# Delta-rule core: decode states by 32-wide TensorE tiles, and three inputs of an iteration made at the end of the one before

## What is computed

```
def step(s, xs):
    qk_i, qd_i, kd_i, u_i, w_i, gt_i = xs
    v_new = u_i - jnp.einsum('bhcd,bhde->bhce', w_i, s)
    o_i = jnp.einsum('bhcd,bhde->bhce', qd_i, s) + jnp.einsum('bhij,bhje->bhie', qk_i, v_new)
    s = s * gt_i[..., None, None] + jnp.einsum('bhcd,bhce->bhde', kd_i, v_new)
    return s, o_i
```

## Time and profile before

| | |
|---|---|
| median of 3 runs | 1932.04 us (1931.34 to 1932.73) |
| the profiled execution: its own time | 1922.21 us |
| its span | 1919.9 us |
| mean granted TensorE clock | 0.913 of 2.4 GHz |
| core stage, first L1028 to last L972 | 311.7 to about 841 us |

### The profile page before, as it was taken

One profiled execution on the slowest core, in us unless ns is written; L12 is line 12 of the kernel. 1 busy time (PEld: TensorE's weight loads), 2 busy tenths in 40 slices (PEclk: granted clock), 3 DMA queues, 4 the chain that ended last, 5 costly groups with the idle time before them and its releaser, 6 DMA issues. The chain is left out here.

```text
span 1919.9 us, 36793 instructions
## 1 busy us (share of the span) xinstructions
PE 1676.9 (87%) x13304; PEld 1389.8 (72%) x13304; DVE 922.1 (48%) x1578; ACT 769.4 (40%) x1572; POOL 210.9 (11%) x396
## 2 busy tenths in 40 slices
PE   4899849998998899979899999788777777899996
PEld 3899837654565566548799998787555556799996
DVE  2776275354434435435455552421556554556631
ACT  2676322334423433443255542331445442455621
POOL 0232000120210212010000000011111100000000
PEclk9899966999899999987999999895788986899998
DMA  7345230122212221242355666444434323355640
GB/s 178 108 135 161 77 102 28 50 69 83 79 37 82 79 61 56 67 115 69 107 139 146 161 164 146 121 139 138 159 104 157 125 94 88 88 153 143 179 121 27
DMA packets 283016, 208.09 MB, mean 108 GB/s; under 512 B 29087, under 2 KB 274751, under 8 KB 282448
## 3 DMA queue, kind: packets, MB, share of 16 engines
q1 hardware_dynamic: 273606, 174.22, 32.5%
q0 software_dynamic: 9248, 31.80, 5.2%
q10 hardware_dynamic: 42, 0.44, 0.1%
HBM read 183.57 MB, written 22.85 MB: 108 GB/s over the span
## 5 line engine op out<-in xcount | busy, mean ns | idle before, releaser
L509 PE MATMUL psum<-h_rounded,weights_low 128*128 128x320 f32 x1248 | 394.3, 316 | 30.0 <-DVE h_low_nsa L420 10.2
L509 PEld LDWEIGHTS psum<-h_rounded,weights_low 128*128 128x128 f32 x1248 | 236.4, 189 | 36.4 <-DVE h_low_nsa L420 10.7
L950 PE MATMUL psum<-sbuf_resident 128*128 128x504 f32 x512 | 254.6, 613 | 0.0
L511 PE MATMUL psum<-h_rounded,weights_high_wide 128*128 128x320 f32 x704 | 219.7, 312 | 0.0
L510 PE MATMUL psum<-h_low_ffn,weights_high_wide 128*128 128x320 f32 x704 | 218.4, 310 | 0.0
L511 PE MATMUL psum<-h_rounded,weights_high 128*128 128x320 f32 x544 | 167.8, 308 | 0.0
L584 DVE SCALAR_TENSOR_TENSOR sbuf_stages<-sbuf_stages,sbuf_resident 128x344 f32<-128x344 f32 (+1 forms) x184 | 105.6, 574 | 110.5 <-ACT sbuf_stages L566 106.6
L485 DVE TENSOR_TENSOR weights_low<-sbuf_resident,weights_high_wide 128x2048 fp32r<-128x2048 f32 (+1 forms) x60 | 149.6, 2499 | 14.5 <-ACT weights_high_wide L470 14.5
L983 ACT COPY sbuf_resident<-psum 64x256 f32<-64x256 f32 x256 | 93.8, 366 | 143.0 <-PE psum L943 140.4
L470 ACT CAST weights_high_wide<-sbuf_resident 128x2048 fp32r<-128x2048 f32 (+1 forms) x60 | 123.6, 2063 | 60.1 <-DMA sbuf_resident<-in_ffn_w_down_dram 60.1
L485 DVE TENSOR_TENSOR weights_low<-sbuf_resident,weights_high 128x2048 fp32r<-128x2048 f32 x46 | 105.1, 2291 | 82.3 <-ACT weights_high L470 82.3
(11 more groups left out here) (410 smaller groups left out, 3229.3 us busy)
## 6 DMA issues: line engine op xcount, KB each, us to landing
sbuf_resident<-in_ffn_w_up_dram SPq DMA_DIRECT2D x88, 512.0 KB, 4.9
sbuf_resident<-in_gdn_w_in_dram SPq DMA_DIRECT2D x48, 512.0 KB, 4.7
sbuf_resident<-in_ffn_w_down_dram SPq DMA_DIRECT2D x32, 704.0 KB, 6.2
sbuf_resident<-in_cache_nsa_kv_dram SPq DMA_DIRECT2D x256, 64.0 KB
sbuf_stages<-in_state_gdn_s_dram POOLq DMA_DIRECT2D x16, 512.0 KB, 5.3
out_gdn_s_sample_dram<-sbuf_stages SPq DMA_DIRECT2D x16, 512.0 KB, 3.5
sbuf_resident<-in_gdn_w_out_dram SPq DMA_DIRECT2D x16, 512.0 KB, 5.5
sbuf_stages<-in_cache_nsa_kv_dram POOLq DMA_DIRECT2D x64, 128.0 KB, 3.5
```

Of the source, the lines that this page charges most:

```text
L509: pe.matmul(out, w_lo, x_hi_tile, start=first, stop=False)
L511: return pe.matmul(out, w_hi, x_hi_tile, start=False, stop=last)
L950: last = pe.matmul(psum[:, H_BANK[t], 0:4 * NC2], w1[:, v, 8 * half + m, t * P:(t + 1) * P], blocks, start=(m == 0 and half == 0), stop=(m ...
```

## The change

Four edits, all in the core:

1. **Old states (L1104, now L1108).** Each 128x128 mask matmul becomes matmuls with 32 stationary columns: for each head, k or q (`x`) and sequences 0 to 3 or 4 to 7 (`e`) have their own quarter of 32 output partitions, and each quarter accumulates four sequences (`b`). 16 matmuls per head where there were 8. The masks shrink from 8 x 64 to 8 x 32 columns for each of k and q.
2. **New states (L1149, now L1154).** `spread` holds on its rows 0 to 31 sequences 0 to 3 and on rows 32 to 63 sequences 4 to 7, 512 columns in place of 1024; the two matmuls of a head use 32 rows each, rows 0 to 31 for one bank, rows 32 to 63 for the other.
3. **ACT copies k and q of iteration i+1 at the end of iteration i**, after the outputs and before the silu; the first pair before the loop. PE's first wait is for q instead of v1, and a wait for v is added before the transposes of v. POOL makes the masks first in its iteration, before the loads of states.
4. **DVE makes the two row products of iteration i+1 in iteration i**, when PE has done the outputs, before the additions of the new states; the first pair before the loop.

```diff
+    put("tok_four", t[:64, None] // TQ % 4 == b[None, :4])
+    put("spare", np.zeros((P, 1468)))
...
-            h["spread"] = space.take(NB, P, off=start)
+            h["spread"] = space.take(NB // 2, P, off=start)
...
-        kqmask = kmask_space.rearrange("p (b x c) -> p b x c", b=NB, x=2)
+        kqmask = kmask_space[:, 0:NB * 2 * 32].rearrange("p (e b x c) -> p e b x c", e=2, b=4, x=2)
...
-            dve=steps("core_dve", both(["row", "bts", "d", "cd", "at1"]) + ["atc", "ya", "yb", "x0"] + both(["at2"])
+            dve=steps("core_dve", both(["bts", "d", "cd", "at1"]) + ["atc", "ya", "yb", "x0"] + both(["at2"])
...
-                      + both(["rs", "vn0", "vns", "s1", "r1", "vn1", "s2"]) + both(["snew"]), lag=True),
-            act=steps("core_act", ["k", "q"] + both(["v"]) + ["ktok"] + both(["egc", "dec", "kdec", "r"]) + both(["qs"]) + both(["o"]), loop=True),
+                      + both(["rs", "vn0", "vns", "s1", "r1", "vn1", "s2", "row"]) + both(["snew"]), lag=True),
+            act=steps("core_act", both(["v"]) + ["ktok"] + both(["egc", "dec", "kdec", "r"]) + both(["qs"]) + both(["o"]) + ["k", "q"], lag=True),
             pool=steps("core_pool", ["kmask", "s0g0", "s0g1", "spread0", "spread1"], lag=True))
...
-            pe.wait_ge(act_steps.sem, act_steps.count("v1", i))
+            pe.wait_ge(act_steps.sem, act_steps.count("q", i - 1))
             pe.wait_ge(dve_steps.sem, dve_steps.count("qkd1", i - 1))
...
-            pe.wait_ge(dve_steps.sem, dve_steps.count("row1", i))
+            pe.wait_ge(dve_steps.sem, dve_steps.all_before(i))
...
+                pe.wait_ge(act_steps.sem, act_steps.count(f"v{h}", i))
                 pe.wait_ge(dve_steps.sem, dve_steps.count(f"p{LEVELS - 1}{h}", i))
...
-                for b in range(NB):
-                    last = pe.matmul(psum[:, B_BANK[h], 3 * P:4 * P], kqmask[:, b].rearrange("p x c -> p (x c)"), hd[h]["S0"][:, b, :],
-                                     start=(b == 0), stop=(b == NB - 1))
+                for b in range(4):
+                    for x in range(2):
+                        for e in range(2):
+                            last = pe.matmul(psum[64 * x + 32 * e:64 * x + 32 * e + 32, B_BANK[h], 3 * P:4 * P], kqmask[:, e, b, x, :],
+                                             hd[h]["S0"][:, 4 * e + b, :], start=(b == 0), stop=(b == 3))
...
                 for x, b in ((0, A_BANK[h]), (1, B_BANK[h])):
-                    last = pe.matmul(psum[:, b, :], d["kdec"][0:TS, 2, :],
-                                     d["spread"][0:TS, 4 * x:4 * x + 4, :].rearrange("p a b -> p (a b)"), start=True, stop=True)
+                    r = slice(32 * x, 32 * x + 32)
+                    last = pe.matmul(psum[:, b, :], d["kdec"][r, 2, :], d["spread"][r].rearrange("p a b -> p (a b)"), start=True, stop=True)
...
-            act.sem_inc(S5["act"].sem, 1)
+            act.sem_inc(S5["act"].sem, S5["act"].first - 2)
...
+            for x in ("k", "q"):
+                take(act, 0, x).then_inc(S5["act"].sem, 1)
...
+        def take(act, i, x):
+            if x == "k":
+                return act.copy(kS[:, 0:T], one(qkv[:, bass.ds(QKH + i, 1), :]))
+            return act.copy(qS, one(qkv[:, bass.ds(i, 1), :]))
+
         def act_core_pair(act, g, i, v):
             act_steps, dve_steps, pe_steps = S5["act"], S5["dve"], S5["pe"]
-
-            act.wait_ge(pe_steps.sem, pe_steps.count("o1", i - 1))
-            act.wait_ge(S5["pool"].sem, S5["pool"].count("kmask", i - 1))
-            act.copy(kS[:, 0:T], one(qkv[:, bass.ds(QKH + i, 1), :])).then_inc(act_steps.sem, act_steps.step("k"))
-            act.copy(qS, one(qkv[:, bass.ds(i, 1), :])).then_inc(act_steps.sem, act_steps.step("q"))
...
+            act.wait_ge(S5["pool"].sem, S5["pool"].count("kmask", i))
+            for x in ("k", "q"):
+                take(act, i + 1, x).then_inc(act_steps.sem, act_steps.step(x))
...
+        def rows_of(dve, i, h):
+            return dve.tensor_scalar(row_src[h], rows4[:, 0:2, :], ident[0:VH, bass.ds(2 * i + h, 1)], None, ALU.mult)
+
         def dve_core(dve):
             dve_steps, pe_steps, act_steps, pool_steps = S5["dve"], S5["pe"], S5["act"], S5["pool"]
-            dve.sem_inc(dve_steps.sem, dve_steps.first)
+            dve.sem_inc(dve_steps.sem, dve_steps.first - 4)
+            for h in range(2):
+                rows_of(dve, 0, h).then_inc(dve_steps.sem, 2)
...
-                for h in range(2):
-                    dve.wait_ge(pe_steps.sem, pe_steps.all_before(i))
-                    dve.tensor_scalar(row_src[h], rows4[:, 0:2, :], ident[0:VH, bass.ds(2 * i + h, 1)], None, ALU.mult).then_inc(dve_steps.sem, dve_steps.step(f"row{h}"))
...
+                    dve.wait_ge(pe_steps.sem, pe_steps.count(f"o{h}", i))
+                    rows_of(dve, i + 1, h).then_inc(dve_steps.sem, dve_steps.step(f"row{h}"))
...
+            pool.wait_ge(act_steps.sem, act_steps.count("q", i - 1))
+            for x, src in ((0, kS), (1, qS)):
+                four = const("col_seq").rearrange("p (b c) -> p b c", b=NB)[:, 0:4, 0:32]
+                last = pool.tensor_tensor(kqmask[:, :, :, x, :], four.unsqueeze(1).to_broadcast([P, 2, 4, 32]),
+                                          src[:, TP:T].rearrange("p (e c) -> p e c", e=2).unsqueeze(2).to_broadcast([P, 2, 4, 32]), ALU.mult)
+            last.then_inc(pool_steps.sem, pool_steps.step("kmask"))
             pool.wait_ge(state_out, STATES * i + 16)
             for h in range(2):
                 pool.dma_start(hd[h]["S0"], st[bass.ds(2 * i + h, 1)].rearrange("o k b v -> (o k) b v")).then_inc(state_in, 16)
-            pool.wait_ge(act_steps.sem, act_steps.count("q", i))
-            for x, src in ((0, kS), (1, qS)):
-                last = pool.tensor_tensor(kqmask[:, :, x, :], const("col_seq").rearrange("p (b c) -> p b c", b=NB),
-                                          src[:, TP:T].unsqueeze(1).to_broadcast([P, NB, TS]), ALU.mult)
-            last.then_inc(pool_steps.sem, pool_steps.step("kmask"))
...
-                pool.tensor_tensor(hd[h]["spread"][0:TS], hd[h]["vn"][0:TS, 2, :].unsqueeze(1).to_broadcast([TS, NB, P]),
-                                   const("tok_seq", TS).unsqueeze(2).to_broadcast([TS, NB, P]), ALU.mult).then_inc(pool_steps.sem, pool_steps.step(f"spread{h}"))
+                pool.tensor_tensor(hd[h]["spread"][0:TS], hd[h]["vn"][0:TS, 2, :].unsqueeze(1).to_broadcast([TS, 4, P]),
+                                   const("tok_four", TS).unsqueeze(2).to_broadcast([TS, 4, P]), ALU.mult).then_inc(pool_steps.sem, pool_steps.step(f"spread{h}"))
```

2 lines of the change are left out of this document (1 added, 1 removed).

## The result

The changed kernel takes 1867.32 us (median of 4 runs, 1863.5 to 1874.97) against 1931.69 us of the kernel before in the same comparison (four runs, 1919.97 to 1932.73). The ratio is 0.9685, with a 95% interval from 0.9637 to 0.9734: faster by 3.2%.

A forecast was written before the change was run, and what follows sets the result against it. PE was taken as the bound, idle only around iteration boundaries. Savings of 12.7, 14.2, 16.3, 3.8 and 3, less 0.3, make 49.7: 1922.2 becomes 1872.5, plus 9.8 gives 1882.3 us, range 1876 to 1896.

The forecast's parts named there:

- term 1: Old states (L1104): four column tiles at once, 1.98 us against 3.57 per iteration, 12.7 us saved; ends -2 to 14.
- term 2: New states (L1149): 32-row matmuls run in pairs, 1.77 us instead of 3.54 per iteration, 14.2 us saved; ends 0 to 14.2.
- term 3: Boundaries without a loop branch, into iterations 1, 3, 5, 7: no wait before the Gram products, 16.3 us saved.
- term 4: Boundaries with the loop branch, into iterations 2, 4, 6: the branch pause stays, 3.8 us saved.
- term 5: First small product to old states (L1054 to L1104): low-clock stretches and port stall mostly go, 3 us saved; ends 0 to 4.
- start and first iteration: Entry of the core stage: first start, like the last end, would move within 1 us.
- A: Old states: column tiles of full height run only two at once, saving about 0 instead of 12.7, total 1895 us; chance 0.09.
- D: Old and new states: small tiles don't overlap at all, old states 30.5 us longer, new states gain nothing, total 1940; chance 0.03.
- rival E: Odd boundaries: PE pauses for code there too, its program being longer, 3.3 us at each of four, total 1895; chance 0.04.
- rival B: Before the first small product (L1054): the ACT–DVE chain holds PE after all, 7.6 + 2.8 us less gain, total 1893; chance 0.14.
- rival C: After boundaries: two more stretches at 1.2 GHz and the last 3 us gain lost, total 1890; chance 0.12.
- the last of the sum: From profiled execution to median: 1872.5 us plus the 9.8 by which the earlier median exceeded its profiled run, giving 1882.3.

The follow-up runs named there:

- e1: Kernel before with only the 32-wide old and new states, halved masks and spread products, nothing moved: 1887.16 us, ratio 0.9818 to the kernel before.
- e4: Changed kernel with PE's eight iterations written out instead of four passes of a loop: 1852.82 us, ratio 0.9611 to the kernel before.
- e7: Kernel before, without the change, with PE's loop over pairs of iterations written out: 1930.5 us, ratio 1.0005 to the kernel before.
- a1: The changed kernel unchanged, timed again: 1867.41 us, ratio 0.9682 to the kernel before.
- e3: Changed kernel with GpSimd's two mask products put back behind the state loads: 1879.34 us, ratio 0.9735 to the kernel before.
- e8: Changed kernel with GpSimd's mask products behind the state loads, the same kernel as e3 run again: 1886.02 us, ratio 0.9785 to the kernel before.
- e2: Kernel before with only the moves (k, q, row products and masks made an iteration earlier), old tiles kept: 1897.44 us, ratio 0.984 to the kernel before.
- a0: The changed kernel unchanged, timed again: 1871.96 us, ratio 0.9718 to the kernel before.
- e5: Changed kernel with the old states' 32 matmuls ordered quarter by quarter: 1897.94 us in one execution.
- e6: Changed kernel with VectorE's two row products put back to the start of the iteration: 1877.5 us, ratio 0.9749 to the kernel before.
- e9: Changed kernel with PE's loop written out, the same kernel as e4 run again: 1853.82 us, ratio 0.9627 to the kernel before.

## Why the prediction was right, and where wrong

| step | predicted | measured in the profiled pair |
|---|---|---|
| term 1, old states | 12.7 | 13.5 (1.69 x8) |
| term 2, new states | 14.2 | 13.8 (1.72 x8) |
| term 3, odd boundaries | 16.3 | 15.9 (87.66 to 64.84, less 4 x 1.72) |
| term 4, even boundaries | 3.8 | 4.3 (73.27 to 63.84, less 3 x 1.72) |
| term 5, L1055 to L1108 | 3 | 2.2 |
| start and first iteration | within 1 | 3.0 |
| L1115 to new states | none | 0.7 |
| end of the stage | -0.3 | 0.0 (1083.30 to 1081.60 for the rest, less 1.72) |
| sum | 49.7 | 53.4 |

**Terms 1 and 2** held: four column tiles of full height run at once, 110 ns for four records. The bound from below by L965's pairs was rightly left; what decided was L1058, four tiles on the diagonal. Rivals A and D are gone. The Trainium skill's 2.38x for three column tiles (TensorE: Matmul & The Clock Gate, Measured speedup vs the span model) is not what four did here: each quarter by its own 109 ns would take 7.0 us for 64 records, and they took 1.88, which is 3.7x.

**Term 3** held to 0.2 us in the piece (16.05 forecast, 16.21 found in all four), and so did its parts: 1.91, 1.01, 2.25 and 11.03 us. The wait before L1029 is gone as said. But the 11.0 us from L1044 to L1055 are not PE's own pace. They hold a wait for ScalarE's turned rows:

```profile
500.21 0.66 PE L944 MATMUL psum<-sbuf_resident 128*128 128x128 f32 x4 [1.28 <-ACT sbuf_resident L984]
```

Even iterations lack it and take 9.75 us where the clock is back by then. That changed nothing here, but it sent 11.0 into term 4. And the stall of the 32-partition products, which I gave to the moved masks, goes in e1 without any move of theirs.

**Term 4** came near its number by two errors against each other. The pause grew from 3.32 to 3.87 us to 3.84 to 4.63, the next piece was 1.3 shorter than I had it, and one boundary in three kept a stretch of 10.2 us at 1.2 GHz. What the prediction said of the mechanism, that the branch stays and is what nobody should hope to lose there, is borne out by e4; but in the kernel before it cost nothing (e7). So rival E, a pause in the straight part too, is refuted (2.93 us at all four odd boundaries), rival B would show as a wait ahead of L1055 in the odd pieces, which are all at 16.21 us, and rival C, more stretches at 1.2 GHz, did not come true in the profiled pair (20.2 us against 47.0), though a1 with 37.4 shows how far it swings.

**The step that failed** is the last of the sum: "the median of the runs is 1932.04, 9.8 more, which I keep". The 1872.5 us of the profiled basis lie 4.1 above the profiled 1868.41, inside the forecast's own spread. But the distance from the profiled run to the median was 9.8 us before and is -1.1 now. It can't be carried over: in the later comparisons 31 runs of the kernel before lie between 1915.65 and 1939.13 with a median of 1929.18, and the three runs shown at first all lay in the upper half, the profiled one in the lower. Its granted clock of 0.913 was near the top of the 0.891 to 0.914 of those 31 (median 0.903); the change's profiled run had 0.911, which is also the median of the change's fifteen. The table of the experiments shows where such a difference sits. The rest of the program has the same instructions in every run, and takes 1077.5 to 1092.2 us, in step with its time at 1.2 GHz, 196 to 251 us; four runs of the change timed with their clocks say the same, 1863.5 at a granted 0.917 and 1874.97 at 0.910. So 10.9 of the 15.0 us come from this step. That it was the clock in the very runs of 1932 us is inferred, since these have no trace. It was also not luck of the draw alone: over all runs the medians lie 58.6 us apart (1929.18 and 1870.56), 5 more than the profiled spans, so a usual execution gains more than the profiled pair shows. The granted clock rose with it, from 0.903 to 0.911 at the median; why, no trace shows, since none was taken of the kernel before at its usual clock.

**The other mis-sized term** is "first start and last end of the stage: within 1 us". It measured 3.0: PE waits 3.34 us in place of 3.99 ahead of the first Gram product and starts 0.7 us sooner, and the clock is back 7 us earlier (314.12 against 321.12), with 2.3 us less from the first Gram product to the first small product. The prediction had looked at GpSimd against VectorE inside the loop and not at the stage's entry. Both halves of the change are needed for it: from the rows to the first small product the first iteration takes 9.75 us with small masks ahead of the loads, 11.63 in e1 and 11.5 in e3 and e8 (small masks behind the loads), and 13.07 in e2 (full masks ahead of them). These go with PE's wait: where it was 3.99 to 4.42 us (before, e7, e1, e2, e3, e8), the clock was back at 320.87 to 324.62; where it was 1.79 to 3.34 (the change, a0, a1, e4, e5, e6, e9), at 312.36 to 314.51.

Last, the range: its lower end of 1876 stood on a single carried offset and had no room for it in the other direction. With 1872.5 and 1882.3 as two equally good readings of the base, it would have had to begin near 1867.

## What to carry to other kernels

Make the sum against the profiled run, and treat the distance from it to the median as a spread on both sides, not as a constant. When two waits lie side by side (here ScalarE's copies and PE's pause at a loop branch), taking one away gains only down to the other: ask for the second one's price, and then remove it as well; here the unrolled loop gave nothing before the change and 14 to 19 us after it. Small column tiles pay when neighbours in program order go to different quarters of the array.

## What the runs showed of the hardware

- Four 32-column tiles of 128 rows run at once: 64 records in 1.88 us. Grouped by quarter, the same records took 4.26 us, less than the 7.0 of a strict row, since a following quarter starts up to some four records early.
- PE's backward branch over this long loop body takes 3.3 to 4.7 us, against 79 to 83 ns for the exit. The Trainium skill (Advanced Engine Details and Errata, Control Flow Timing) has about 108 ns for a compare-and-branch; only the exit is near that, and with the loop written out no such gap appears.
- After such a pause, the same instructions on the same data got the 1.2 GHz level for 3.4, 6.8, 10.2 or 13.7 us in different executions; the piece behind it takes 9.8 or 13.0 us accordingly.
- VectorE's 32-partition products of two SBUF inputs were held beside GpSimd's masks, which read SBUF (up to 3.79 us for one, 0.35 otherwise), and not beside its state loads (1.44 us for four).
- Single executions far off the rest occurred: one of 2703 us (e8) and one of 8277 us (e9), each in six runs. No trace shows what they were.
